# The MLP by half-size products: where raw weights are held, and when the first pair's pieces are formed

## The chip, the core and the metric

The kernel runs on one core of a Trainium2 chip. The core has TensorE (PE), VectorE (DVE), ScalarE (ACT), GpSimd (POOL) and SyncE (SP), each with a queue of its own that is worked off in order, and 16 DMA engines. The metric is the device time of one execution in microseconds. Most executions of a kernel agree within 0.3%.

## The reference, cut to what matters

The program computes two transformer layers with attention and then a block with three mixers. Only its last part is touched by the change: the feed-forward part of the last block, on 512 tokens of width 1024, with an inner width of 4096, all in float32.

```python
h = rmsnorm_2(x, norm_mlp_w[l]) * (1.0 + sc2) + sh2
ff = jnp.square(jax.nn.relu(h @ mlp_w1[l])) @ mlp_w2[l]      # mlp_w1 1024 x 4096, mlp_w2 4096 x 1024
x = x + g2 * ff
return rmsnorm_2(x, final_norm_w)
```

## The kernel before

**Numbers.** Every float32 operand is held as a high part (a copy to fp32r) and a low part (the float32 value minus the high part). A product is three matmuls for each tile: high by high, high by low and low by high. For weights, ACT writes the high part (`wH` for a unit, `pieceH` for a piece) and POOL the low one (`wL`, `pieceL`); DVE writes the low part of some pieces. A low part waits for its high part.

**Units.** A unit is 128 columns of a weight matrix, eight tiles of 128 x 128, loaded as 512 KB. Its raw form lies in one of the two halves of `w32`, by turns, and SP asks for unit u when unit u-2 is split (the semaphore `w_lo` counts split units). Split units lie in 4 slots. ACT and POOL split three units ahead of PE. The matmuls of a unit write a PSUM bank, `G[0]` or `G[1]` by turns.

**The feed-forward part.** It runs in four quarters c = 0 to 3 of 1024 inner columns each. A quarter has eight steps n, one for each unit of the first matrix (units 8c to 8c+7). In a step, PE multiplies unit n. Then ACT takes the relu of the bank, DVE squares it, which gives the bank free (`f_sq`), and forms sums of squares, ACT writes high parts (`hi1`, `sumH`), and POOL and DVE write low parts (`lo1`, `sumL`). PE's unit n+2 needs the bank of unit n.

Then the quarter's product with the second matrix follows by a scheme with seven half-size products for each pair of output columns, where eight would be usual. A pair q (4 a quarter, 15 in all; the last two column blocks are multiplied as ordinary units 32 and 33) is two raw blocks of 512 KB. Seven pieces are formed from them, in the order A11, S1, S2, S4, A12, S3, A22, and held in 10 places by turns. S1, S2 and S4 are formed by DVE in PSUM (`sum_1`, `sum_2`, `sum_4` into banks `O` and `N`), S3 by POOL into `third` (the tile `rms`). ACT writes each piece's high part, POOL the low part of A11, A12, S3 and A22, DVE that of S1, S2 and S4. Raw pairs lie in `wp` (even q) and in `w32` (odd q). In PE's order of a quarter, `first_tiles`, the first three products are `product_1(q)`, `product_5(q)` and `product_1(q + 1)`, then `product_6(q)`. `product_1` takes A11, `product_6` takes S2 and adds into the bank of `product_1`. Before it adds, DVE must have read the bank (`take`, which adds a product to `xT`). At the quarter's end the first half of unit 8 is multiplied between two products of the last pair.

**What sets the order.** The order on each engine is the order of the code in the functions `quarter` and `pieces` of SP, POOL, ACT and DVE; no planner changes it. Before the change, steps 0 to 4 of a quarter end with the split of unit n+3, and steps 5 to 7 end with the pieces of the quarter's first pair. The pieces of pair q+1 begin after step 7. On SP, `quarter` asks for the raw pairs, and for the next quarter's units only when the last pair is split. In quarter 0, DVE has in each step also an `ada_block` (a product with 1024 columns of the modulation matrix, raw in `adaw`, line L1104), and after step 7 the last of these and the sum into `modT`, by which `take` scales.

## Time and profile before

| | us |
|---|---|
| median of 3 runs | 1303.78 (1303.32 to 1304.76) |
| the profiled execution | 1303.05 |
| its span | 1301.3 |
| PE busy | 1237.2 (95%) |
| DVE busy | 813.2 (62%) |
| ACT busy | 718.3 (55%) |
| POOL busy | 448.8 (34%) |
| mean granted clock of TensorE | 0.977 of full speed |

The feed-forward part takes the last third of the span, from about 890 us. Its quarters begin (first matmul of unit 8c) at about 890, 992.4, 1091.5 and 1190.4 us. In a row of a timeline the number in brackets at the end is the time for which the engine stood still before that instruction, and behind the arrow stands what ended it. PE's starts are the better measure of its pace, since matmuls overlap. The times of one execution stand in its rows, so they are compared with its own 1303.05 us.

### The profile page before, as it was taken

What the parts mean: (1) busy time and instruction counts of PE and PEld (TensorE: products, weight loads), DVE (VectorE), ACT (ScalarE), POOL (GpSimd) and SP (SyncE); (2) the same over time, 40 slices, a digit from 0 to 9 for tenths busy, and PEclk for the clock granted to TensorE, in tenths of its full rate; (3) what the DMA queues carried; (4) which work ended last, traced back from release to release, by engine and by line L of the source; (5) the groups of instructions that cost most, each with busy time, mean ns of one, the idle gap of its engine ahead of it and who ended that gap; (6) DMA issues with size and microseconds to landing.
All of it is one profiled execution on the core that took longest, in us unless ns stands there. A gap on an engine that the chain in (4) does not pass through costs nothing.

```text
span 1301.3 us, 20815 instructions
## 1 busy us (share of the span) xinstructions
PE 1237.2 (95%) x7638; PEld 1021.3 (78%) x7638; DVE 813.2 (62%) x1735; ACT 718.3 (55%) x1405; POOL 448.8 (34%) x284
## 2 busy tenths in 40 slices
PE   9999999999999998999999999999878978978977
PEld 8777777778877776896767888889778878878877
DVE  6766667765766666656995466847763453453456
ACT  6666666655456676445678867435422532432432
POOL 0000000005200000434877841233854655655653
PEclk9999999999999999999999999999989989989989
DMA  5312244425232223423220223321512312312311
GB/s 201 115 65 82 81 162 129 129 85 172 86 107 88 82 84 112 139 89 105 73 74 29 71 75 105 130 96 62 199 65 83 113 66 81 113 66 81 113 66 65
DMA packets 38420, 128.21 MB, mean 99 GB/s; under 512 B 4640, under 2 KB 7584, under 8 KB 38320
## 3 DMA queue, kind: packets, MB, share of 16 engines
q1 hardware_dynamic: 35792, 121.91, 28.1%
q10 hardware_dynamic: 2528, 4.98, 1.1%
q8 instruction: 61, 1.00, 0.3%
q14 instruction: 39, 0.32, 0.1%
HBM read 123.43 MB, written 2.13 MB: 96 GB/s over the span
## 4 chain that ended last, share of the span: by engine, by line
PE 71%; issue 8%; DVE 7%; ACT 7%; POOL 5%; DMA 0%; ACTq 0%; DVEq 0%; POOLq 0%
PE G L987 14%; PE G L989 13%; PE G L988 13%; ACT scr L1368 2%; POOL pieceL L634 2%; PE G L2049 2%; PE S L1826 2%; PE G L2050 2%; PE G L2051 2%; PE S L1114 2%; PE O L1175 2%; POOL wL L572 1%; PE T L1154 1%; DVE wL L2761 1%; ACT wH L2198 1%
## 5 line engine op out<-in xcount | busy, mean ns | idle before, releaser
L572 POOL TENSOR_TENSOR wL<-w,wH 128x1024 fp32r<-128x1024 f32 x89 | 216.9, 2442 | 668.0 <-ACT wH L2198 668.0
L987 PE MATMUL G<-hi,wH 128*128 128x512 f32 x968 | 394.8, 408 | 12.0 <-POOL wL L572 11.6
L989 PE MATMUL G<-hi,wL 128*128 128x512 f32 x968 | 380.5, 393 | 0.0
L988 PE MATMUL G<-lo,wH 128*128 128x512 f32 x968 | 380.4, 393 | 0.0
L987 PEld LDWEIGHTS G<-hi,wH 128*128 128x128 f32 x968 | 183.1, 189 | 58.9 <-POOL wL L572 12.7
L989 PEld LDWEIGHTS G<-hi,wL 128*128 128x128 f32 x968 | 183.3, 189 | 40.3
L988 PEld LDWEIGHTS G<-lo,wH 128*128 128x128 f32 x968 | 183.7, 190 | 35.6 <-issue 1.2
L2198 ACT ACTIVATE wH<-w 128x1024 fp32r<-128x1024 f32 x140 | 147.2, 1053 | 101.8 <-DMA w<-weights_dram 72.8
L2761 DVE TENSOR_TENSOR wL<-w,wH 128x1024 fp32r<-128x1024 f32 x51 | 62.3, 1221 | 42.3 <-ACT wH L2198 41.5
L2667 ACT ACTIVATE pieceH<-O 128x512 fp32r<-128x512 f32 x30 | 18.0, 598 | 110.6 <-DVE O L3298 58.7
L3311 DVE SCALAR_TENSOR_TENSOR xT<-G,modT,xT 128x256 f32<-128x256 f32 x60 | 28.9, 482 | 78.6 <-PE G L2051 78.6
L2050 PE MATMUL G<-sumL,pieceH 128*128 128x256 f32 x180 | 52.5, 292 | 0.0
L2051 PE MATMUL G<-sumH,pieceL 128*128 128x256 f32 x180 | 52.4, 291 | 0.0
L2049 PE MATMUL G<-sumH,pieceH 128*128 128x256 f32 x180 | 52.4, 291 | 0.0
L2049 PE MATMUL G<-hi,pieceH 128*128 128x256 f32 x60 | 19.8, 329 | 33.6 <-POOL pieceL L634 32.5
L1142 ACT ACTIVATE scr<-scr,sa 128x256 f32<-128x256 f32 (+2 forms) x64 | 35.2, 557 | 23.7 <-DVE sa L1129 23.7
L1104 DVE CUSTOM_DVE_ANT_0 adaw<-adaw,scr 128x1024 f32<-128x1024 f32 x31 | 45.2, 1457 | 4.3 <-issue 4.0
L1368 ACT ACTIVATE scr<-S,bs,bq 128x128 f32<-128x128 f32 (+1 forms) x64 | 33.6, 534 | 21.7 <-DVE bs L1358 21.7
L634 POOL TENSOR_TENSOR pieceL<-wp,pieceH 128x512 fp32r<-128x512 f32 x24 | 35.3, 1469 | 25.9 <-ACT pieceH L2667 25.9
L646 POOL TENSOR_TENSOR sumL<-sq,sumH 128x256 fp32r<-128x256 f32 (+1 forms) x32 | 33.4, 1046 | 27.5 <-ACT sumH L2706 18.7
L634 POOL TENSOR_TENSOR pieceL<-w,pieceH 128x512 fp32r<-128x512 f32 x21 | 27.5, 1311 | 43.2 <-ACT pieceH L2667 43.2
L2703 ACT ACTIVATE relu<-G 128x512 f32<-128x512 f32 x31 | 18.5, 597 | 40.9 <-PE G L989 37.6
(553 smaller groups left out, 2784.6 us busy)
## 6 DMA issues: line engine op xcount, KB each, us to landing
w<-weights_dram SPq DMA_DIRECT2D x154, 512.0 KB, 3.7
adaw<-ada_dram SPq DMA_DIRECT2D x43, 512.0 KB, 4.1
wp<-weights_dram SPq DMA_DIRECT2D x16, 512.0 KB, 4.6
kd<-c_dram ACTq DMA_DIRECT2D x8, 512.0 KB, 3.7
cbias<-ada_dram SPq DMA_DIRECT2D x5, 512.0 KB, 4.4
xT<-x_dram SPq DMA_DIRECT2D x4, 512.0 KB, 7.8
out_dram<-xT SPq DMA_DIRECT2D x8, 256.0 KB, 2.3
scr<-ca_dram SPq DMA_DIRECT2D x2, 512.0 KB, 5.0
```

What stands on the lines that cost most here:

```text
L572: g.tensor_tensor(wL[:, u.slot], w32[:, u.slot % 2], wH[:, u.slot].bitcast(f32), ALU.subtract).then_inc(w_lo, 1)
L634: g.tensor_tensor(pieceL[:, piece(q, i)], home, pieceH[:, piece(q, i)].bitcast(f32), ALU.subtract).then_inc(piece_lo_g, 1)
L987: mm(home[:, :], whi, H[:, k, :], start=(k == first), stop=False)
L988: mm(home[:, :], whi, L[:, k, :], start=False, stop=False)
L989: last = mm(home[:, :], wlo, H[:, k, :], start=False, stop=(k == final))
L1104: v.tensor_tensor_reduce(out=home, in0=home, in1=copy, scale=1.0, scalar=0.0, op0=ALU.mult, op1=ALU.add, accum_out=modsum[:, b.n:b.n + 1]) ...
L1368: s.activation(pb[:, h * 512 + at:h * 512 + at + w], S[h][:, at:at + w], ACT.Exp, bias=st[:, NEGM, h, q:q + 1], scale=bq[:, n % 2, ROOT, h ...
L2049: mm(home, pieceH[:, at, k, :], high, start=first and k == 0, stop=False, skip_group_check=True)
L2050: mm(home, pieceH[:, at, k, :], low, start=False, stop=False, skip_group_check=True)
L2051: last = mm(home, pieceL[:, at, k, :], high, start=False, stop=(k == 3), skip_group_check=True)
L2198: s.activation(wH[:, u.slot], w32[:, u.slot % 2], ACT.Copy).then_inc(w_hi, 1)
L2761: v.tensor_tensor(wL[:, u.slot], w32[:, u.slot % 2], wH[:, u.slot].bitcast(f32), ALU.subtract).then_inc(w_lo, 1)
```

## The change

Units and pairs share both raw buffers. From quarter 1 on, units 0, 1, 4 and 5 of a quarter lie in `wp`, and units 2, 3, 6 and 7 in `w32`. Where SP waited for the last pair of a quarter to be split and then asked for five units, it now asks for units 8 and 9 when pair q+2 (in `wp`) is split, for 10 and 11 when pair q+3 is split, for 12 and 13 when unit 9 is split and for 14 and 15 when unit 11 is. Pair q of the next quarter follows when its unit 5 is split and pair q+1 when unit 7 is. The semaphores that announce raw data follow the buffer.

(The last hunk is DVE's, at the end of each step.) In a step, the split of unit n+3 stands before the sums' parts: on ACT just behind the relu, on POOL first. The pieces of the first pair are formed in steps 2 to 5, where they were in steps 5 to 7, and A11, S1's and S2's sums of pair q+1 in step 6. At a quarter's end ACT splits units 8, 9 and 10 behind the last piece as before, and in quarter 3 ahead of three squares of the final norm. PE's order is unchanged.

```diff
+        def raw_home(u):
+            c, n = divmod(u.n - UM, 8) if isinstance(u.n, int) else (0, 0)
+            if 0 < c < 4:
+                return (w32 if n // 2 % 2 else wp)[:, n % 2]
+            return w32[:, u.slot % 2]
...
+            def pair_split(q):
+                sp.wait_ge(*mark("piece_sum", 3 * q + 3))
+                sp.wait_ge(*mark("piece_lo_g", 4 * q + 4))
+
             def load_pair(q):
-                if q > 1:
-                    sp.wait_ge(*mark("piece_sum", 3 * (q - 2) + 3))
-                    sp.wait_ge(*mark("piece_lo_g", 4 * (q - 2) + 4))
...
             def quarter(c):
-                for n in range(5, 8):
-                    load_unit(Unit(UM + 8 * c + n))
-                    if c == 0:
-                        load_ada(Block(ADA_M, n - 3))
-                if c == 0:
-                    sp.wait_ge(*mark("lo_mlp", 16))
-                load_pair(4 * c)
+                first = UM + 8 * c
                 if c == 0:
                     for n in range(5, 8):
+                        load_unit(Unit(first + n))
+                        load_ada(Block(ADA_M, n - 3))
+                        if n == 5:
+                            sp.wait_ge(*mark("lo_mlp", 16))
+                            load_pair(0)
+                    for n in range(5, 8):
                         load_ada(Block(ADA_M, n))
-                sp.wait_ge(w_lo, UM + 8 * c + 8)
+                else:
+                    sp.wait_ge(w_lo, first + 6)
+                    load_pair(4 * c)
+                sp.wait_ge(w_lo, first + 8)
                 load_pair(4 * c + 1)
+                pair_split(4 * c)
                 load_pair(4 * c + 2)
-                if c < 3:
-                    load_pair(4 * c + 3)
-                sp.wait_ge(*mark("piece_sum", 3 * (4 * c + 3 - 2 * (c == 3)) + 3))
-                sp.wait_ge(*mark("piece_lo_g", 4 * (4 * c + 3 - 2 * (c == 3)) + 4))
-                for n in range(5 if c < 3 else 2):
-                    load_unit(Unit(UM + 8 * c + 8 + n))
+                pair_split(4 * c + 1)
...
+                load_pair(4 * c + 3)
+                pair_split(4 * c + 2)
+                load_later(first + 8)
+                load_later(first + 9)
+                pair_split(4 * c + 3)
+                load_later(first + 10)
+                load_later(first + 11)
+                sp.wait_ge(w_lo, first + 10)
+                load_later(first + 12)
+                load_later(first + 13)
+                sp.wait_ge(w_lo, first + 12)
+                load_later(first + 14)
+                load_later(first + 15)
...
-                    if n == 5:
+                    if n == 2:
                         sum_1(q)
                         sum_2(q)
-                    if n == 6:
+                    if n == 3:
                         low_of(q, S1)
+                    if n == 4:
                         sum_4(q)
                         low_of(q, S2)
-                    if n == 7:
+                    if n == 5:
                         low_of(q, S4)
+                    if n == 6:
+                        sum_1(q + 1)
+                        sum_2(q + 1)
...
                 take(q, A11)
-                sum_1(q + 1)
                 take(q, S1)
-                sum_2(q + 1)
```

On POOL this is the place from the sums of unit 5 to the second pair, in quarter 1. `sumL` and `lo<-sq` are the low parts of sums for a unit, `pieceL<-wp` those of pair q's A11, A12 and A22, `pieceL<-w` those of pair q+1, and `rms` is S3's sum. Before:

```order
L646 TENSOR_TENSOR sumL<-sq,sumH 128x256
L646 TENSOR_TENSOR sumL<-sq,sumH 128x2x256
L634 TENSOR_TENSOR pieceL<-wp,pieceH 128x512
L640 TENSOR_TENSOR rms<-wp 128x512
L646 TENSOR_TENSOR lo<-sq,hi 128x256
L634 TENSOR_TENSOR pieceL<-wp,pieceH 128x512
L646 TENSOR_TENSOR sumL<-sq,sumH 128x256
L646 TENSOR_TENSOR sumL<-sq,sumH 128x2x256
L634 TENSOR_TENSOR pieceL<-rms,pieceH 128x512
L634 TENSOR_TENSOR pieceL<-wp,pieceH 128x512
L634 TENSOR_TENSOR pieceL<-w,pieceH 128x512
L640 TENSOR_TENSOR rms<-w 128x512
```

And now:

```order
L692 TENSOR_TENSOR sumL<-sq,sumH 128x256
L692 TENSOR_TENSOR sumL<-sq,sumH 128x2x256
L680 TENSOR_TENSOR pieceL<-rms,pieceH 128x512
L680 TENSOR_TENSOR pieceL<-wp,pieceH 128x512
L692 TENSOR_TENSOR lo<-sq,hi 128x256
L680 TENSOR_TENSOR pieceL<-w,pieceH 128x512
L692 TENSOR_TENSOR sumL<-sq,sumH 128x256
L692 TENSOR_TENSOR sumL<-sq,sumH 128x2x256
L686 TENSOR_TENSOR rms<-w 128x512
L680 TENSOR_TENSOR pieceL<-w,pieceH 128x512
```

A11 and the S3 sum of pair q are gone from here to steps 2 and 3, and `pieceL<-w`, A11 of pair q+1, stands ahead of the two `sumL` of unit 7, where it stood as the third instruction behind them.

On ACT this is step 2 and what follows it, in quarter 1, beginning with the relu of unit 2. `wH` is a unit's high part, `hi<-T` and `hi<-sq` are those of the squares and their sums, and `pieceH` those of A11 (from `wp`) and S1 (from bank `O`). Before:

```order
L2703 ACTIVATE relu<-G 128x512
L2714 ACTIVATE hi<-T 128x256
L2715 ACTIVATE hi<-sq 128x256
L2198 ACTIVATE wH<-w 128x1024
L2703 ACTIVATE relu<-G 128x512
L2706 ACTIVATE sumH<-sq 128x256
L2708 ACTIVATE hi<-T 128x512
L2709 ACTIVATE sumH<-sq 128x2x256
L2198 ACTIVATE wH<-w 128x1024
L2703 ACTIVATE relu<-G 128x512
```

And now:

```order
L2752 ACTIVATE relu<-G 128x512
L2248 ACTIVATE wH<-wp 128x1024
L2765 ACTIVATE hi<-T 128x256
L2766 ACTIVATE hi<-sq 128x256
L2717 ACTIVATE pieceH<-wp 128x512
L2717 ACTIVATE pieceH<-O 128x512
L2752 ACTIVATE relu<-G 128x512
L2248 ACTIVATE wH<-w 128x1024
L2757 ACTIVATE sumH<-sq 128x256
L2759 ACTIVATE hi<-T 128x512
L2760 ACTIVATE sumH<-sq 128x2x256
L2717 ACTIVATE pieceH<-N 128x512
```

The unit's high part moved up behind the relu, and the high parts of A11 and S1 of pair q stand between unit 2's sums and the relu of unit 3.

## Rows read from the trace of the kernel before

**Rows 1.** Chain that ended last, of the page, shares of the span by engine.

```profile
PE 71%; issue 8%; DVE 7%; ACT 7%; POOL 5%; DMA 0%; ACTq 0%; DVEq 0%; POOLq 0%
```

**Rows 2.** Waits of PE from 850 us on: waited for, us in total, times, longest us.

```profile
PE G L2049 <- POOL pieceL L634: 32.5, 4, 10.1
PE G L987 <- POOL wL L572: 11.6, 4, 3.5
PE G L2049 <- DVE lo L3343: 1.0, 1, 1.0
PE G L2167 <- POOL wL L572: 1.0, 1, 1.0
```

**Rows 3.** Timeline of PE: start us, us, line, out<-in, idle before and its releaser.

```profile
950.53 0.58 PE L2049 MATMUL G<-hi,pieceH 128*128 128x256 f32 x1 [10.06 <-POOL pieceL L634]
...
992.43 0.50 PE L987 MATMUL G<-hi,wH 128*128 128x512 f32 x1 [3.41 <-POOL wL L572]
...
1091.49 0.50 PE L987 MATMUL G<-hi,wH 128*128 128x512 f32 x1 [3.53 <-POOL wL L572]
```

**Rows 4.** Windows of PE: us, busy, granted clock PEclk, DMA share, GB/s.

```profile
952.00:954.00 2.00, 2.00 (x11) 0.50 0.47 190
```

**Rows 5.** Timeline of PE, single matmuls of the second pair's stage and of quarter 1.

```profile
953.25 0.41 PE L2049 MATMUL G<-sumH,pieceH 128*128 128x256 f32 x1
...
1022.15 0.39 PE L987 MATMUL G<-hi,wH 128*128 128x512 f32 x1
...
1039.16 0.28 PE L2049 MATMUL G<-hi,pieceH 128*128 128x256 f32 x1
...
1040.60 0.28 PE L2049 MATMUL S<-hi,pieceH 128*128 128x256 f32 x1
...
1095.94 0.28 PE L2049 MATMUL G<-sumH,pieceH 128*128 128x256 f32 x1
```

**Rows 6.** Timeline of ACT in quarter 1, units 2, 3, 5, 6 and 7.

```profile
1012.15 0.60 ACT L2703 ACTIVATE relu<-G 128x512 f32<-128x512 f32 x1 [0.89 <-PE G L989]
...
1014.62 1.05 ACT L2198 ACTIVATE wH<-w 128x1024 fp32r<-128x1024 f32 x1
...
1017.59 0.60 ACT L2703 ACTIVATE relu<-G 128x512 f32<-128x512 f32 x1 [1.93 <-PE G L989]
...
1034.76 0.60 ACT L2667 ACTIVATE pieceH<-O 128x512 fp32r<-128x512 f32 x1 [2.17 <-DVE N L3292]
1035.26 0.59 ACT L2703 ACTIVATE relu<-G 128x512 f32<-128x512 f32 x1
...
1040.34 0.59 ACT L2703 ACTIVATE relu<-G 128x512 f32<-128x512 f32 x1
```

**Rows 7.** Timeline of POOL: a unit's low part, and a quarter's last piece.

```profile
1015.74 2.39 POOL L572 TENSOR_TENSOR wL<-w,wH 128x1024 fp32r<-128x1024 f32 x1 [0.20 <-ACT wH L2198]
...
1082.90 1.29 POOL L634 TENSOR_TENSOR pieceL<-w,pieceH 128x512 fp32r<-128x512 f32 x1
```

**Rows 8.** The pair loads' line on SP, time from issue to landing.

```profile
DMA to landing us min/median/max: 3.5/4.5/6.8
```

**Rows 9.** Timeline of DVE: quarter 0's last ada block and modT, then quarter 1.

```profile
944.76 1.70 DVE L1104 CUSTOM_DVE_ANT_0 adaw<-adaw,scr 128x1024 f32<-128x1024 f32 x1
...
946.51 1.10 DVE L3359 TENSOR_TENSOR modT<-modsum,vecT 128x8 f32<-128x8 f32 x1
...
1032.20 1.80 DVE L3288 TENSOR_TENSOR O<-wp 128x512 f32<-128x512 f32 x1
...
1040.97 0.70 DVE L3327 TENSOR_TENSOR T<-relu,G 128x512 f32<-128x512 f32 x1 [1.08 <-ACT relu L2703]
...
1043.44 0.69 DVE L3334 TENSOR_TENSOR lo<-T,hi 128x512 fp32r<-128x512 f32 x1 [0.66 <-ACT hi L2708]
...
1044.65 0.47 DVE L3311 SCALAR_TENSOR_TENSOR xT<-G,modT,xT 128x256 f32<-128x256 f32 x1
1045.04 0.80 DVE L3288 TENSOR_TENSOR O<-w 128x512 f32<-128x512 f32 x1
```

More of the change, by code:

```diff
@@ L348, in pair_home, with pair_raw, raw_here @@
             return w32 if q % 2 else wp
+        def pair_raw(eng, q):
+            for n in range(2):
+                if q % 2:
+                    eng.wait_ge(w_here[n], 16 * (58 + q // 4 * 4 + q % 4 // 2))
+                else:
+                    eng.wait_ge(*mark(f"pair_here{n}", 16 * (1 + q // 4 * 4 + q % 4 // 2)))
+        def raw_home(u):
[3 more added lines that the diff above has]
+            return w32[:, u.slot % 2]
+        def raw_here(u):
+            c, n = divmod(u.n - UM, 8) if isinstance(u.n, int) else (0, 0)
+            if c == 4:
+                return w_here[n], 16 * 71
+            if c > 0 and n // 2 % 2 == 0:
+                return mark(f"pair_here{n % 2}", 16 * (4 * c - 1 + n // 4))
+            if c > 0:
+                return w_here[n % 2], 16 * (56 + 4 * c + n // 4)
+            return w_here[u.slot % 2], u.of_pair * 16 + 16
         def piece(q, i):
@@ L647, in sum_low, with rest @@
                                 ALU.subtract).then_inc(f_sum_lo, 1)
-            def pieces(q):
-                low_of(q, A11, pair_home(q)[:, 0, 0:4])
+            def rest(q):
                 third_sum(q)
@@ L658, in quarter @@
                 for n in range(8):
+                    if n < 5:
+                        split_lo(Unit(UM + 8 * c + 3 + n))
                     if n % 2 == 0:
@@ L2679, in third_high, with rest @@
                 high_of(q, S3, third)
-            def pieces(q):
-                raw_high(q, A11)
+            def rest(q):
                 sum_high(q, S1)
@@ L2715, in quarter @@
                         s.activation(sum_home(c, 1, k), raw_sum[:, 0, :], ACT.Copy).then_inc(sem("f_sum_hi"), 1)
[L2716 to L2718 removed]
+                    if n == 2:
                         raw_high(q, A11)
                         sum_high(q, S1)
[L2721 removed]
+                    if n == 3:
                         sum_high(q, S2)
+                    if n == 4:
                         sum_high(q, S4)
                         raw_high(q, A12)
[L2725 removed]
+                    if n == 5:
                         third_high(q)
                         raw_high(q, A22)
[L2728 removed]
+                    if n == 6:
+                        raw_high(q + 1, A11)
+                rest(q + 1)
                 if c == 3:
                     square_f(0, multiplied(q, A12))
[L2731 removed]
+                raw_high(q + 2, A11)
+                rest(q + 2)
+                if c < 3:
+                    raw_high(q + 3, A11)
+                    rest(q + 3)
+                for n in range(2 if c == 3 else 3):
+                    split_hi(Unit(UM + 8 * c + 8 + n))
                 if c == 3:
@@ L2735, in quarter @@
                     square_f(3, multiplied(q + 1, A22))
-                else:
-                    pieces(q + 3)
-                for n in range(2 if c == 3 else 3):
-                    split_hi(Unit(UM + 8 * c + 8 + n))
             for c in range(4):
```

55 lines of the change are left out of this document (31 added, 24 removed).

## Prediction

> **What bounds the kernel now.** I read the chain of waits first. Matmuls hold 71% of it, and the rest is "issue", ACT, DVE and POOL [rows 1]. TensorE (PE) sets the time, and what can be won are the places where it stands still. The list of PE's waits shows them for the whole feed-forward part [rows 2]: 32.5 us in four waits for POOL's `pieceL`, 11.6 us in four waits for POOL's `wL`, and 1.0 us twice. A reader should see that seven of these ten come at two places that return in each quarter. PE's own timeline gives the places [rows 3]. The wait that ends at 950.53 stands before `product_1(q+1)`, the first product of a quarter's second pair, after two products of the first pair. Those that end at 992.43 and 1091.49 stand before unit 8 of a quarter, which is unit 0 of the next. In all, the waits are 32.5 + 11.6 + 1.0 + 1.0 = 46.1 us.
>
> They cost more than their length. After the wait of 10.06 us the granted clock is 0.50 [rows 4], which is 1.2 GHz of 2.4. At full clock the twelve matmuls of a product take 1.44 us (1039.16 to 1040.60), and after the wait they take 2.72 (950.53 to 953.25) [rows 3, 5], so 1.3 is lost there and about 1.0 in the next product's time, until the clock is back near 955.6. I use 2.3 for each of the four. After the boundary wait, the 12 matmuls from 1091.49 to 1095.94 take 4.45 us [rows 3, 5], where 12 of the 24 in a unit of 5.44 us (the relus of units 2 and 3 lie 1012.15 to 1017.59 [rows 6]) take 2.72: 1.7 lost, three times. Together the stalls cost 46.1 + 4 x 2.3 + 3 x 1.7 = 60.4 us. That is all that the edits can win, since no matmul is removed.
>
> **What the change removes.** The piece wait first. POOL's low part of A11 of pair q+1 now stands in step 6, ahead of unit 7's sums. The sum for S1 and S2 of that pair stands in step 6 on DVE. So `product_1(q+1)` finds its weights. The boundary wait: units 8 and 9 go to the buffer of the pair before last and are asked for when that pair is split, not after the quarter's last piece. Now POOL goes straight from its last piece to `split_lo(8)`. At the second boundary this piece ends at 1084.2 (1082.90 + 1.29) and a split takes 2.4 [rows 7], so 1086.6, and PE is there at 1088.0 (1091.49 - 3.53), 1.4 us later. So all of the 3.4 us goes, at each of the three boundaries. Unit 3's wait in quarter 0 (1.3, the rest of the 11.6) goes because its copies now precede the sums of step 0. The 1.0 at the end of quarter 3 goes for the same reason.
>
> **What it adds in quarters 1 to 3.** Buffer `wp` holds units 4 and 5 of the quarter until unit 5 is split, in step 2. Only then may pair q be asked for, and step 2 ends by waiting for it, on ACT, DVE and POOL alike. These queues are in order: the relu of unit 3 stands behind the pieces on ACT, and the unit 3 square that frees the bank for unit 5 stands behind the sums on DVE. Step by step in quarter 1: relu(2) starts 1012.15; the next ACT start is 0.50 later, the copy takes 1.05 [rows 6]; POOL's subtract takes 2.39 [rows 7], to 1016.2. Loads of pairs landed 4.5 us after their issue at the median [rows 8], so the pair is here at 1020.7. `sum_1` takes 0.80 or, beside a POOL instruction, 1.80 [rows 9]; POOL waits for ACT here, so I take 0.80, to 1021.5. `sum_2` about 0.7, the high part of S1 0.50 to the next start [rows 6], so relu(3) starts at 1022.8 instead of 1017.59. The square starts 0.63 after its relu and takes 0.70 [rows 6, 9], so G[1] is free at 1024.15. Unit 5 started at 1022.15 [rows 5]. The stall is 2.0 us, and with a `sum_1` of 1.80 it is 3.0. The load's own bounds are 3.5 and 6.8 us [rows 8]: 1.0 with the fast sum, 5.3 with the slow one. Does 2.0 lower the clock? In the trace the waits of 1.0 did not and that of 3.41 did, as the 4.45 us for twelve matmuls show [rows 2, 3, 5]. I take 0.5 of the 1.7. Steps 3 to 6 then catch up, since a relu may be some 4 us late before a bank is missed.
>
> The next thing late is `product_6(q)`. It adds into the bank that `take(q, A11)` must have read, and this stands behind unit 7's squares, sums and low part on DVE. A relu that is free starts about 0.9 after its unit's last matmul is out (unit 5 follows at 1022.15, relu(4) is due at 1017.59 + 5.44), so relu(7) stands at 1040.05 for a `product_1(q)` at 1039.16. The low part starts 3.1 later (1040.34 to 1043.44 [rows 6, 9]), the take 0.6 behind it, and it is done 0.47 after that: 1044.2. Three products of 1.44 from 1039.16 end at 1043.5. The stall is 0.9, and I allow 0.7 to 1.3. The longer piece wait had covered it. Per quarter 2.0 + 0.5 + 0.9 = 3.4, three times 10.2.
>
> From there on each piece follows a take that follows a product, as before, at the same distances from PE. There is no PE wait in that phase before [rows 2], so nothing more is paid there.
>
> **What it adds in quarter 0.** Here pair q is loaded early, but every step also has an ada block on DVE (1.70 us for one of them [rows 9]). Pair 1's load stands on SP behind the ada load that waits for block 5. Carrying the durations above through steps 2 to 6 with one such block in each, I put block 5's end at 932.5, pair 1 at 938.2, relu(7) at 938.7, and after two sums of DVE its square at 940.7. So `product_1(q+1)` starts at 940.8, 2.5 us late, and `product_1(q)` was 1.1 late. Unit 7's sums and low part end at 943.2, the ada block at 944.6, `modT` (1.10 [rows 9]) and the take at 946.4. `product_6(q)` starts at 946.5, against 953.25 before [rows 5]: 6.75 us gained of 13.5 (1.3 + 1.0 + 10.06 + 1.1 of low clock). The idle gap of 8 us in two parts will lower the clock again, about 2 us. So 6.75 + 2.0 = 8.75 us stays.
>
> **The sum.** 60.4 - 10.2 - 8.75 = 41.45 us. The profiled execution took 1303.05 us for a span of 1301.3 (1.75 around it), and 1303.05 - 41.45 = 1261.6. The median of the runs, 1303.78, is 0.7 above that execution, so 1262.3, rounded to 1262.
>
> **A rule weighed against the rows.** `sum_1` took 1.80 us at one place, where a POOL subtract ran beside it, and 0.80 at another [rows 9]. The Trainium skill, GPSIMD Engine Reference, section Specifications, says that POOL shares its SBUF interfaces with VectorE and contends with vector instructions that have two SBUF inputs. `sum_1` is such an instruction, and the trace agrees. By that rule alone every moved `sum_1` would cost 1.80, and the time would be 3 us longer, 1265. In the new order POOL's next instruction needs ACT's copy first, so it stands still just then, and the sum above keeps 0.80.
>
> **The rivals.** *A, the raw pair arrives late for step 2.* For it: three engines end step 2 in that wait, one of them with the relu of the next unit behind it. Against it: two banks give slack. With the 6.8 us load and the 1.80 sum the stall is 5.3, and it lowers the clock for 1.7: (5.3 + 1.7 - 2.5) x 3 = 13.5 us more, 1276. *B, nothing new is late.* If ACT and DVE find the pair at once and quarter 0 keeps its order better than I reckon, only the take remains, 3 x 0.9 plus some 3 us in quarter 0: 60.4 - 6 = 54 us gained, 1249. For it: a bank is missed only if its relu is over 4 us late, and the load alone is that long. Against it: the load cannot be asked for before unit 5's split. *C, slower than before: the steps run at ACT's and DVE's pace.* Each hands the other a bank (`first_bank`, `second_bank`), so steps 2 to 6 each may last as their exchange. A step of that kind was long: relu(6) came at 1035.26 [rows 6], where steps of 5.44 from 1017.59 give 1033.9, so it lasted 6.8. At 6.8 five steps cost 6.8 us per quarter, mostly hidden by the slack. It decides against the change when a step passes 8.5 us, since 5 x 3.1 x 4 = 62 us then eat all 60.4; at 9.0 us a step, 72 - 60 = 12 us slower, 1315. Against it: the ada blocks that would make steps so long exist in quarter 0 alone. *D, it doesn't remove the piece wait*, because another input of `product_1(q+1)`, the square of unit 7, comes late too: it ended at 1041.7 (1040.97 + 0.70 [rows 9]), and `product_1(q+1)` is due at 1042.0 (1040.60 + 1.44 [rows 5]). D costs nothing as long as relu(7) is on time, but relu(7) now stands behind pair q+1's load. If that load is 3 us late, each of four quarters gives 3 us back, 1274.
>
> **How the numbers follow.** Forecast 0.52 (1254 to 1269), A 0.20, D 0.10, B 0.13, C 0.05. The range reaches to B's edge and past A: 1249 to 1281. A measurement here tells 0.2% (2.6 us) from no change. All but C lie more than 20 us below, so faster 0.94, same 0.02, slower 0.04.
>
> **What would show it.** Right: no PE wait before `product_1` of pairs 5, 9, 13 nor over 0.5 us at a boundary; a wait of about 2 us before unit 5 of quarters 1 to 3 whose last releaser is DVE's square, with ACT idle before the high part of A11 until the load lands; a wait of about 1 us before `product_6(q)` on DVE's `xT`; some 7 us in quarter 0 around 937 to 947; granted clock 1.00 through nearly all pair stages. Wrong: a wait over 5 us at step 2 or 3 (A), or a `relu` spacing above 8 us in steps 2 to 6 (C), or waits for `wL` at boundaries as before.

## Result and profile after

| | before | after |
|---|---|---|
| median, us | 1304.27 (1303.32 to 1305.66, 4 runs) | 1262.6 (1261.96 to 1264.08, 4 runs) |
| the profiled execution | 1303.05 | 1261.96 |
| its span | 1301.3 | 1260.2 |
| PE busy | 1237.2 | 1226.8 |
| mean granted clock | 0.977 | 0.996 |

The ratio is 0.9681, with a 95% interval of [0.9665, 0.9698]: 41.7 us faster. PE executes the same 7638 matmuls in both; it is busy 10.4 us less because it runs at full clock for longer.

The chain that ended last in the changed kernel, against [rows 1]:

```profile
PE 75%; ACT 7%; DVE 7%; issue 6%; DMA 2%; POOL 1%; SPq 0%; ACTq 0%; DVEq 0%; POOLq 0%
```

The matmuls' share rose from 71% to 75% and POOL's fell from 5% to 1%. DMA is new with 2%, the raw pair for which step 2 now waits. The waits of PE from 850 us on, against [rows 2] (waited for, us in total, times, longest us):

```profile
PE G L1037 <- DVE T L3381: 6.5, 5, 1.7
PE G L2099 <- issue: 4.3, 3, 3.5
PE G L2099 <- POOL pieceL L680: 2.5, 1, 2.5
PE G L2099 <- DVE lo L3397: 1.6, 1, 1.6
```

46.1 us of waits became 14.9. L1037 was L987, and L2099 was L2049. No wait for `wL` is left, and one for `pieceL`, in quarter 0. PE's timeline says where these 14.9 us lie, against [rows 3] (in brackets the wait, and what ended it):

```profile
939.25 0.36 PE L2099 MATMUL G<-hi,pieceH 128*128 128x256 f32 x1 [1.62 <-DVE lo L3397]
...
945.12 0.52 PE L2099 MATMUL G<-hi,pieceH 128*128 128x256 f32 x1 [2.45 <-POOL pieceL L680]
...
951.49 0.36 PE L2099 MATMUL G<-sumH,pieceH 128*128 128x256 f32 x1 [3.49 <-issue]
...
1018.00 0.47 PE L1037 MATMUL G<-hi,wH 128*128 128x512 f32 x1 [1.52 <-DVE T L3381]
...
1104.09 0.47 PE L1037 MATMUL G<-hi,wH 128*128 128x512 f32 x1 [1.71 <-DVE T L3381]
```

The first three are quarter 0: before `product_1(q)`, `product_1(q+1)` and `product_6(q)`. The last two are unit 5 of quarters 1 and 2 (quarter 3 has one of 1.56). `product_6(q)` waits 0.47 in quarter 2 and 0.38 in quarter 3. Quarter 0 has two more for a bank, 0.33 before unit 3 (908.49) and 1.34 before unit 5 (920.96). Where the profile names "issue" for `product_6`, DVE's rows below show what it waited for.

The clock, in windows of PE (us, busy, granted clock, DMA share, GB/s), against [rows 4]:

```profile
946.00:948.00 2.00, 1.99 (x10) 0.50 0.00 0
...
952.00:954.00 2.00, 2.00 (x11) 0.50 0.00 0
...
1016.00:1018.00 2.00, 0.48 (x4) 1.00 0.00 0
1018.00:1020.00 2.00, 2.00 (x9) 1.00 0.00 0
```

In quarter 0 the clock falls to 0.50 (1.2 GHz) twice. Around the wait of 1.52 in quarter 1 it stays at 1.00 (2.4 GHz), and so it does at every wait of quarters 1 to 3.

By the spacing of the relus of units 8c (ACT's timeline; the last stage ends with the span), in us:

| stage | before | after | gained | forecast |
|---|---|---|---|---|
| quarter 0 and its boundary | 99.60 | 92.14 | 7.46 | 11.05 |
| quarter 1 | 99.06 | 85.91 | 13.15 | 11.4 |
| quarter 2 | 98.90 | 86.57 | 12.33 | 11.4 |
| quarter 3 to the end | 102.07 | 92.97 | 9.1 | 7.6 |

The forecast column divides the prediction's own terms: waits and clock of a stage, less 3.4 a quarter or 8.75 in quarter 0. The relu of unit 0 stands 0.94 us later than before (902.61 against 901.67), in code that the change does not touch. It lay between 900.8 and 904.8 in the profiled executions of this study, so a difference of up to 4 us between single spans need not be the effect of an edit. From that relu on, two profiled executions of the changed kernel lasted 357.6 and 358.5 us, 0.9 apart. The experiments below are compared by medians, by PE's waits, and where it matters by the span from that relu on.

### The profile page after: what moved, and what is told of

It reads as the page before. It is cut to its first block, busy times and chain, and to the rows that moved or that the text cites. A ratio compares the mean times of both kernels' runs of the same rounds, so it can differ in the third digit from the quotient of the medians.

```text
span 1260.2 us, 20816 instructions
## 1 busy us (share of the span) xinstructions
PE 1226.8 (97%) x7638; PEld 1010.3 (80%) x7638; DVE 816.9 (65%) x1735; ACT 716.3 (57%) x1405; POOL 447.7 (36%) x284
## 4 chain that ended last, share of the span: by engine, by line
PE 75%; ACT 7%; DVE 7%; issue 6%; DMA 2%; POOL 1%; SPq 0%; ACTq 0%; DVEq 0%; POOLq 0%
PE G L1037 14%; PE G L1039 13%; PE G L1038 13%; PE G L2099 2%; PE G L2100 2%; PE G L2101 2%; ACT scr L1418 2%; PE S L1164 2%; PE O L1225 2%; PE S L1876 1%; PE T L1204 1%; ACT wH L2248 1%; DVE wL L2815 1%; PE S L2100 1%; PE S L2101 1%
## 5 line engine op out<-in xcount | busy, mean ns | idle before, releaser
L618 POOL TENSOR_TENSOR wL<-w,wH 128x1024 fp32r<-128x1024 f32 x77 | 189.7, 2468 | 678.0 <-ACT wH L2248 677.9
L1037 PE MATMUL G<-hi,wH 128*128 128x512 f32 x968 | 393.0, 406 | 6.9 <-DVE T L3381 6.5
L1037 PEld LDWEIGHTS G<-hi,wH 128*128 128x128 f32 x968 | 182.1, 188 | 54.5 <-issue 18.6
L2248 ACT ACTIVATE wH<-w 128x1024 fp32r<-128x1024 f32 x128 | 134.7, 1054 | 80.5 <-DMA w<-weights_dram 48.9
L2099 PE MATMUL G<-sumH,pieceH 128*128 128x256 f32 x180 | 51.5, 286 | 4.4 <-issue 4.3
L1154 DVE CUSTOM_DVE_ANT_0 adaw<-adaw,scr 128x1024 f32<-128x1024 f32 x31 | 48.2, 1555 | 1.9 <-issue 1.8
L2099 PEld LDWEIGHTS G<-sumH,pieceH 128*128 128x128 f32 x180 | 34.7, 193 | 5.3 <-issue 5.2
```

Of the source, the lines that this page charges most:

```text
L618: g.tensor_tensor(wL[:, u.slot], raw_home(u), wH[:, u.slot].bitcast(f32), ALU.subtract).then_inc(w_lo, 1)
L1037: mm(home[:, :], whi, H[:, k, :], start=(k == first), stop=False)
L1154: v.tensor_tensor_reduce(out=home, in0=home, in1=copy, scale=1.0, scalar=0.0, op0=ALU.mult, op1=ALU.add, accum_out=modsum[:, b.n:b.n + 1]) ...
L2099: mm(home, pieceH[:, at, k, :], high, start=first and k == 0, stop=False, skip_group_check=True)
L2248: s.activation(wH[:, u.slot], raw_home(u), ACT.Copy).then_inc(w_hi, 1)
```

## The experiments

The theory is the prediction's: the gain is the sum of three separate waits, each with a loss of clock behind it, and what remains is one wait per quarter for the raw pair, with quarter 0 on DVE's pace. The rival is that the waits overlap, or that one of the edits does nothing. "After" means the changed kernel, 1262.6 us. Each ratio is to the kernel before, with its 95% interval.

**The second pair's pieces back behind step 7.**

```diff
-                    if n == 6:
-                        low_of(q + 1, A11, pair_home(q + 1)[:, 0, 0:4])
+                low_of(q + 1, A11, pair_home(q + 1)[:, 0, 0:4])
                 rest(q + 1)
...
-                    if n == 6:
-                        raw_high(q + 1, A11)
+                raw_high(q + 1, A11)
                 rest(q + 1)
...
-                    if n == 6:
-                        sum_1(q + 1)
-                        sum_2(q + 1)
...
                 take(q, A11)
+                sum_1(q + 1)
                 take(q, S1)
+                sum_2(q + 1)
```

> The changed kernel, but A11 and the sums for S1 and S2 of pair q+1 are formed after step 7 again. Theory 1 (the step-6 pieces remove the piece wait): in quarters 1 to 3 POOL's low part of A11 ends some 4.2 us after product_1(q+1) is due, and this covers the wait of about 0.45 us before product_6; with about 2.3 us of low clock that makes 3 x 6 = 18 us, and quarter 0 about 0, since relu(7) is then free of pair 1's load: 1281 us. Rival (the gain came from the shared raw buffers and the earlier unit copies): under 2 us more, 1264 us at most.

Measured: 1276.91 us (1276.15 to 1277.45), ratio [0.9782, 0.9814]. PE's waits and its clock at the one in quarter 1:

```profile
PE G L2098 <- POOL pieceL L680: 15.6, 4, 4.1
```

```profile
1038.00:1040.00 2.00, 1.35 (x6) 0.50 0.00 0
```

The wait is back in all four quarters, 3.8 to 4.1 us each, and the clock falls at each of them. It takes 14.3 us from the gain: 13.1 us more of waits for pieces, 4.3 less before `product_6` (the longer wait covers it), and the rest is clock. The wait is not 8.1 us as before, since the first pair's pieces now stand in steps 2 to 5 and POOL, ACT and DVE come to the second pair sooner.

The expectation was 1281, and the 4 us between lie in quarter 0. By the spacing of the relus, quarters 1 to 3 took 6.2, 5.5 and 5.8 us longer than in the changed kernel, 17.5 in all where 18 were expected; quarter 0 took 89.42 us where the changed kernel took 92.14, 2.7 less. So the second pair's pieces in step 6 are worth 17.5 us in quarters 1 to 3 and cost 2.7 in quarter 0, where the relu of unit 7 stands behind the pair's late load. No run kept them in step 6 for quarters 1 to 3 alone.

**The next quarter's units asked for only behind the last piece.**

```diff
                 pair_split(4 * c + 2)
-                load_later(first + 8)
-                load_later(first + 9)
                 pair_split(4 * c + 3)
+                load_later(first + 8)
+                load_later(first + 9)
```

> The changed kernel, but units 8 and 9 are asked for only when the quarter's last pair is split. Theory 1 (the earlier request removes the wait at the boundary): POOL's last piece ends 3.0 us before PE needs unit 8, landing 3.7, copy 1.06, low part 2.4 make a wait of 4.2 us, and 1.7 us of low clock, three times: 1280 us. Rival (PE is held at the boundary by something else, or the slack of 1.4 us that was forecast was not real): under 5 us more in all.

Measured: 1280.87 us (1279.75 to 1281.27), ratio [0.9809, 0.9842]. The waits:

```profile
PE G L1037 <- POOL wL L618: 10.4, 3, 3.6
```

The boundary waits are back as they were, and the clock falls at each, 18.3 us in all. So the earlier request is worth about 6 us a boundary, where the prediction had 3.4 + 1.7 = 5.1. The waits before unit 5 and in quarter 0 are 0.7 us longer here too, and the last of the three falls of the clock lasted longer than the other two.

**A step's copies for unit n+3 back at its end.**

```diff
                 for n in range(8):
-                    if n < 5:
-                        split_lo(Unit(UM + 8 * c + 3 + n))
                     if n % 2 == 0:
                         sum_low(c, n // 2, 1)
...
                         sum_low(c, n // 2, 2)
                         sum_low(c, n // 2, 3, 2)
+                    if n < 5:
+                        split_lo(Unit(UM + 8 * c + 3 + n))
```

That is POOL's part; on ACT `split_hi` moves in the same way behind the step's high parts.

> The changed kernel, but unit n+3 is split behind the sums of its step again. Theory 1 (in steps 2 of quarters 1 to 3 PE waits for the chain unit 5's split, pair load, sums, relu of unit 3): the split ends 1.75 us later, so the wait before unit 5 grows from 1.5 to 3.3 us, and a clock drop of 1.7 may follow: 5 to 10 us more and 1 us in quarter 0, 1269 to 1274 us. Rival (moved copies only matter for unit 3 of quarter 0): 1263.6 us.

Measured: 1276.88 us (1275.78 to 1279.59), ratio [0.9789, 0.9821], 3 us above the expected range. PE's waits, then the one of quarter 1 and the clock around it:

```profile
PE G L1037 <- DVE T L3381: 12.3, 4, 3.9
...
PE G L1037 <- POOL wL L618: 2.5, 2, 1.3
```

```profile
1022.39 0.76 PE L1037 MATMUL G<-hi,wH 128*128 128x512 f32 x1 [3.44 <-DVE T L3381]
```

```profile
1022.00:1024.00 2.00, 1.61 (x4) 0.50 0.00 0
```

The waits grew as expected: raw unit 5 is split later, the pair is asked for later, and unit 5's product waits 3.4 to 3.9 us where it waited 1.5 to 1.7. The clock, which the expectation had as a possibility, falls at each of the three; after 1.5 to 1.7 us it stays at 1.00. The upper end of the expectation already holds these falls at 1.7 us each. What lies above it is spread: the three waits grew by 6.2 us and not by 5.4, the second of the falls lasted longer than the other two, and quarter 0 took 2.1 us more by its relus and not 1, with waits of 1.30 and 1.19 for `wL`. So this edit, which looks like a detail, is worth 14 us, mostly because it keeps the new wait short and the clock up.

**The first pair's pieces one step later in quarters 1 to 3** (steps 3 to 6 in place of 2 to 5), on POOL, ACT and DVE:

```diff
+LATER = 1
...
-                    if n == 2:
+                    m = n - LATER if c else n
+                    if m == 2:
                         low_of(q, A11, pair_home(q)[:, 0, 0:4])
-                    if n == 3:
+                    if m == 3:
...
```

> The changed kernel, but in quarters 1 to 3 the first pair's pieces are formed in steps 3 to 6, not 2 to 5. Theory 1 (ACT and DVE hold unit 3's relu and square while they wait for the pair's load): the pair lands about 0.4 us before relu(3)'s step ends, so the three waits of 1.5 to 1.7 us before unit 5 go, 4.8 us in all, and POOL has 4.6 us of work in step 6, less than a step of 5.44: 1258 us. Rival (POOL or ACT has no room in step 6, so the wait moves to product_1(q+1)): 1262 to 1266 us.

Measured: 1256.39 us (1255.08 to 1260.07), ratio [0.9622, 0.9675], 6.2 us less than after. Its waits of PE:

```profile
PE G L2101 <- issue: 4.6, 1, 4.6
PE G L2101 <- POOL pieceL L681: 2.4, 1, 2.4
```

These two, 1.6 before `product_1(q)` and 1.6 in quarter 0's first steps are all that is left of the waits of the feed-forward part, and they lie in quarter 0. In quarters 1 to 3 no wait of PE is listed, neither before unit 5 nor before `product_6`, and no new one came. ACT and DVE have the same work in these quarters as before the edit. So the wait before unit 5 was the raw pair's landing inside step 2 and not their pace (rival C): the relus of units 2 and 3 of quarter 1, which lay 10.9 us apart, now lie 5.44 apart. By the relus, quarters 1 to 3 are 1.8, 2.45 and 2.1 us shorter than in the changed kernel, 6.3 in all, which is what its waits there cost.

**The last ada block and `modT` in step 6 of quarter 0, ahead of the second pair's sums.**

```diff
+                    if c == 0 and n == 6:
+                        ada_block(dve, Block(ADA_M, 7))
+                        dve.wait_ge(sem("ada_summed"), 48)
+                        link(v.tensor_tensor(modT[:, 40:48], modsum[:, 40:48], vecT[:, 40:48], ALU.add))
...
-                if c == 0:
-                    ada_block(dve, Block(ADA_M, 7))
-                    dve.wait_ge(sem("ada_summed"), 48)
-                    link(v.tensor_tensor(modT[:, 40:48], modsum[:, 40:48], vecT[:, 40:48], ALU.add))
```

> The changed kernel, but in quarter 0 DVE does the last ada block and modT in step 6, ahead of the sums of pair 1, where it stands still for 2.7 us waiting for that pair. Theory 1 (product_6 of pair 0 waits for the take, which stands behind the ada block and modT): the take comes 3.5 us sooner, while the sums of pair 1 come up to 0.5 us later: 3 us less, 1259.6 us. Rival (product_6 waits for the low sums of POOL): no change, 1262.6 us.

Measured: 1258.89 us (1257.07 to 1262.48), ratio [0.9641, 0.9682]. The wait before `product_6` in quarter 0 fell from 3.49 to 0.90:

```profile
948.45 0.55 PE L2099 MATMUL G<-sumH,pieceH 128*128 128x256 f32 x1 [0.90 <-issue]
```

The work fits into time in which DVE stood still: the changed kernel's DVE was idle for 2.74 us before `sum_1` of pair 1. Where it stood, the block and `modT` took 2.30 and 1.10 us, and here 1.59 and 0.17, and `sum_1` still waits 1.04 us for the pair. The last section has what made them slow.

**The take of A11 ahead of unit 7's low part, in quarters 1 to 3.**

```diff
+TAKE_C = 1
...
+                        if n == 7 and TAKE_C <= c:
+                            take(q, A11)
                         dve.wait_ge(sem("f_hi"), 8 * c + n + 1)
...
-                take(q, A11)
+                if c < TAKE_C:
+                    take(q, A11)
```

> The changed kernel, but in quarters 1 to 3 DVE takes A11's product between unit 7's sums and its low part, where DVE stands still 0.67 us for ACT. Theory 1 (product_6 waits for that take): the waits of 0.4 to 0.5 us before product_6 go, 1 us or a little more in all: 1261.5 us. Rival (it waits for the unit's low part or for POOL): 1262.6 us or more. The difference is near what 3 rounds can tell, so the wait in the trace decides.

Measured: 1261.21 us (1260.24 to 1263.04), ratio [0.9655, 0.9701]. The waits before `product_6` in quarters 2 and 3 are gone from PE's timeline. By the median it is 1.4 us less; the intervals of the two ratios overlap, so the time alone does not show it.

**Pair 1 asked for ahead of ada block 7's load in quarter 0.**

```diff
-                    for n in range(5, 8):
+                    for n in range(5, 7):
                         load_ada(Block(ADA_M, n))
...
                 load_pair(4 * c + 1)
+                if c == 0:
+                    load_ada(Block(ADA_M, 7))
```

> The changed kernel, but in quarter 0 SP asks for pair 1 ahead of the last ada load. Theory 1 (relu(7) of quarter 0 stands behind the high part of A11 of pair 1, whose load stands behind an ada load that waits for block 5): pair 1 is here some 6 us sooner, relu(7) comes at about 939.5 and not 943.5, the wait of 2.5 us before product_1(1) goes, and the one before product_6(0) stays near 3 us, as the take moves with relu(7): 3 to 4 us less, 1259 us. Rival (DVE's own work in step 6 sets relu(7)'s square): under 1 us.

Measured: 1260.71 us (1259.74 to 1261.95), ratio [0.9654, 0.9697]. The relu of unit 7 came earlier, and the time before `product_6` was longer:

```profile
940.31 0.59 ACT L2754 ACTIVATE relu<-G 128x512 f32<-128x512 f32 x1
```

```profile
950.13 0.55 PE L2101 MATMUL G<-sumH,pieceH 128*128 128x256 f32 x1 [4.68 <-issue]
```

After, this relu stood at 943.53. Counted from each execution's relu of unit 0 (903.55 here, 902.61 after), it comes 4.2 us earlier, as expected. But the median fell by 1.9 us only, under the 3 to 4 expected: PE did not wait before `product_1(q+1)`, but 1.2 us longer before `product_6`, because DVE still has the ada block and `modT` in front of the take.

**Three of these together** (one step later, the take, pair 1's load):

> The changed kernel with three edits together: pieces one step later in quarters 1 to 3, the take ahead of unit 7's low part there, and pair 1's load ahead of the last ada load. If theory 1 holds they add up: 4.8 + 1.2 + 3.5 = 9.5 us less, 1253 us. If the waits hide one another, less than the largest alone gives and a new wait shows in the trace.

Measured: 1254.6 us (1252.1 to 1256.8), ratio [0.9598, 0.9651]. From the relu of unit 0 on the span is 9.7 us shorter than after, and alone the three edits gave 5.6 (one step later), 3.2 (pair 1's load) and 0.9 (the take) by the same measure: they add up.

**Work in the place of a wait.** The next two ask about the clock alone. The kernel before, with extra matmuls whose results are not used:

```diff
+            def filler(q, count, bank):
+                for n in range(count):
+                    mm(bank[:, HALF[0]], pieceH[:, piece(q, A11), n % 4, :], hi1[:, n % 4, HALF[0]], start=True, stop=True)
...
                 product_5(q)
+                filler(q, 76 if c == 0 else 56, S[1])
                 product_1(q + 1)
```

> The kernel before, with extra matmuls of 256 columns (into a bank of PSUM that is free there; their results are not used, the output stays as it was) between product 5 of a pair and product 1 of the next: 76 in quarter 0 (about 9.1 us of TensorE at full clock) and 56 in each of quarters 1 to 3 (about 6.7 us), so that TensorE computes while the next pair's pieces are late. The four waits for POOL's pieces (8.1 us each before) shrink to what the extra matmuls leave, the pieces come as late as before. Theory 1 (a wait of this length costs its length and then some 2.3 us more, through a granted clock of .50 when TensorE starts again): the clock stays at 1.00 at the four places and the run takes 4 x 2.2 = 9 us less than the kernel before, about 1294.5 us, though TensorE has more to do. Rival (the clock falls there for another cause, or the slow stretch costs nothing because something else is late): no gain, 1303 us or more.

Measured: 1294.72 us (1293.77 to 1296.12) against 1303.82 for the kernel before, measured beside it, ratio [0.9922, 0.9954]. The waits, the second pair's first matmul in quarter 0, and the clock there, where the kernel before has 0.50 [rows 4]:

```profile
PE G L987 <- POOL wL L572: 10.7, 4, 3.2
PE G L2049 <- POOL pieceL L634: 3.6, 4, 1.3
```

```profile
949.72 0.39 PE L2049 MATMUL G<-hi,pieceH 128*128 128x256 f32 x1 [1.04 <-POOL pieceL L634]
```

```profile
952.00:954.00 2.00, 2.00 (x20) 1.00 0.04 12
```

244 more matmuls, 9.1 us faster. The waits for pieces fell by 28.9 us and the extra work is about 29.3 us (0.12 each), so nothing was gained there. The clock stayed at 1.00 at all four places, and the 9.1 us are what four falls of the clock cost: 2.3 us each, or 1.5 to 2.5 by the ends of the ratio's interval. That is the prediction's term, and here it is taken by itself, but for the boundaries: their waits were 0.9 us less in all, and the clock was low for longer behind one of them. The Trainium skill, TensorE: Matmul & The Clock Gate, section Part 1: The HAM clock gate, puts the penalty of the ramp from the low to the full clock under 1% of a typical kernel's span. For the four falls taken away here this run agrees (0.6%, by its interval 0.5 to 0.8%). With the three at the boundaries, 14.3 us by the prediction's terms, it is an estimated 1.1% of this kernel, the size of a real edit.

The three edits together, with 34 such matmuls before `product_6` in quarter 0:

> The three edits of x9 together, and before product 6 of pair 0 in quarter 0, where x9 still waits 4.7 us and then runs at a clock of .50, 34 extra matmuls of 256 columns (4.1 us at full clock, results not used, output unchanged). Theory 1 (the wait lowers the clock): the wait becomes work, the clock stays at 1.00 and 1.5 to 2 us are saved: 1253 us against x9's 1254.6. Rival (the clock falls anyway): no difference from x9, 1254.6 us. If the extra matmuls end after the piece arrives: up to 0.5 us slower than theory 1 says.

Measured: 1251.9 us (1250.99 to 1254.73), ratio [0.9595, 0.9626]. In the trace the wait is 0.66 in place of 4.69:

```profile
949.20 0.36 PE L2104 MATMUL G<-sumH,pieceH 128*128 128x256 f32 x1 [0.66 <-issue]
```

The clock behind the place of the wait, here and then without the extra matmuls, where the wait ended at 951.36:

```profile
950.00:952.00 2.00, 2.00 (x19) 1.00 0.00 0
```

```profile
952.00:954.00 2.00, 2.00 (x11) 0.50 0.00 0
```

The medians differ by 2.7 us, but they were not measured side by side, and their ratios' intervals overlap. From the first of PE's waits in quarter 0, the same instruction in both (it ended at 910.66 and 908.42), to the end the spans are 342.0 and 340.8, 1.3 us less, somewhat under the 1.5 to 2 expected. The direction agrees with the theory; the time does not prove it, the clock's rows do.

**The changed kernel once more,** as the measure for the two with extra matmuls:

> The changed kernel once more, as it is, on the same chip as the two with extra matmuls, so that they are compared in one call: 1262.6 us as before, within 1.5 us.

Measured: 1263.61 us (1262.63 to 1265.05), ratio [0.968, 0.9712]. That is 1.0 us above its first median.

**One step later, the take, and the last ada block in step 6:**

> Three edits together that were run singly: the pieces of the first pair one step later in quarters 1 to 3 (alone 1256.4 us, 6.2 less than the change), the product's take ahead of unit 7's low part (alone 1261.2, 1.4 less), and in quarter 0 the last ada block with modT in step 6 (alone 1258.9, 3.7 less). Theory 1 (the four waits of quarter 0 and the ones of quarters 1 to 3 are separate, so the gains add): 1262.6 - 6.2 - 1.4 - 3.7 = 1251.3 us, and where single runs' errors of about 1 us each overstate them, up to 1253; no wait of PE of 2 us or more but the one before product 1 of pair 1 (2.6). Rival (the gains overlap, or ada block 7 in step 6 delays unit 7 so that its loss shows once the rest is gone): 1254.5 us or more, with a wait over 3 us before product 1 or product 6 in quarter 0.

Measured: 1252.77 us (1250.35 to 1254.22), ratio [0.9593, 0.962]. The waits of PE that are left, 6.8 us, all in quarter 0:

```profile
PE G L2102 <- POOL pieceL L682: 2.8, 1, 2.8
...
PE G L2102 <- issue: 0.8, 1, 0.8
```

The gains add up again within their errors: 9.8 us by the medians, where the single medians sum to 11.3, and 9.6 from the relu of unit 0 on, where they sum to 8.7 (5.6, 0.9 and 2.2). This version has no extra matmuls, and is 50.7 us faster than the kernel before (1303.51, measured beside it).

The three edits of the change do not add up in this way. Taken back singly they cost 14.3, 18.3 and 14.3 us, 46.9 in all, more than the 41.7 that they brought together. The first two remove waits of the kernel before. The third mostly keeps a wait short that the first two brought with them.

## Why the prediction was right, and where its sizes were off

The forecast was 1262.0 and the runs gave 1262.6. The mechanism held in quarters 1 to 3 and in the main in quarter 0, but two terms were off in opposite directions and made up for each other; that the sum came so close is luck.

*What bounds the kernel.* Right. The time lies in PE's waits and the clock behind them. The clock's share, 2.3 us for each wait for a piece, was worked out from two rows; the extra matmuls measured it as 9.1 us for four (6.0 to 10.2).

*What the change removes.* Right but for quarter 0's first steps. No wait before `product_1(q+1)` in quarters 1 to 3, none at a boundary. The wait for `wL` before unit 3 of quarter 0, 1.29 before, is gone as forecast, but 0.33 for a bank is left there, and 1.34 before unit 5 is new. POOL goes from the last piece to the split of unit 8 without a gap (start us, us, then [rows 7]'s columns):

```profile
982.67 1.30 POOL L680 TENSOR_TENSOR pieceL<-w,pieceH 128x512 fp32r<-128x512 f32 x1
983.93 4.78 POOL L618 TENSOR_TENSOR wL<-wp,wH 128x1024 fp32r<-128x1024 f32 x2
```

*The wait for the raw pair in step 2.* Right in its chain, a little large in its size. The same rows of quarter 1 as the prediction built them from [rows 6 to 9], now with the pair's request on SP:

```profile
1005.63 0.60 ACT L2752 ACTIVATE relu<-G 128x512 f32<-128x512 f32 x1 [1.83 <-PE G L1039]
...
1014.56 0.63 ACT L2717 ACTIVATE pieceH<-wp 128x512 fp32r<-128x512 f32 x1 [6.37 <-issue]
...
1016.53 0.59 ACT L2752 ACTIVATE relu<-G 128x512 f32<-128x512 f32 x1
```

```profile
1007.25 2.41 POOL L618 TENSOR_TENSOR wL<-wp,wH 128x1024 fp32r<-128x1024 f32 x1 [1.08 <-ACT wH L2248]
```

```profile
1009.69 0.80 SPq L555 DMA_DIRECT2D wp<-weights_dram  x2
```

```profile
1014.57 0.70 DVE L3342 TENSOR_TENSOR O<-wp 128x512 f32<-128x512 f32 x1 [6.22 <-DMA wp<-weights_dram]
1015.30 0.70 DVE L3346 TENSOR_TENSOR N<-O,wp 128x512 f32<-128x512 f32 x1
...
1017.15 0.70 DVE L3381 TENSOR_TENSOR T<-relu,G 128x512 f32<-128x512 f32 x1 [1.15 <-ACT relu L2752]
```

ACT and DVE both stand still until the pair has landed, 4.9 us after its request, and the relu of unit 3, PE's bank, follows behind them: PE starts unit 5 at 1018.00, when DVE's square is out. ACT's row says "issue", and only DVE's names the DMA: the releaser of a wait is to be read on the engine that shows it. From relu(2) to `sum_1` it took 8.94 us where the prediction had 8.55, and `sum_1` took 0.70 in step 2 of all three quarters, about the 0.80 that the prediction chose, and not the 1.80 of the rule that it weighed, since POOL had nothing to do there. In step 6 POOL was at work, and there `sum_1` took 1.09, 3.07 and 0.91. The stall is 1.5 to 1.7 and not 2.0. It does not touch the clock, where the prediction took 0.5. And `product_6` waits 0, 0.47 and 0.38 and not 0.9 (the prediction's own 1044.2 less 1043.5 is 0.7): in quarter 1 relu(7) started 0.2 us after `product_1(q)`, at 1034.63, where the prediction had 0.9; in quarter 2 the `sum_1` of 3.07 stood before unit 7's square. So the term of 10.2 us measured 5.6 by the waits (1.52 + 1.71 + 1.56 + 0.47 + 0.38), and 6.3 by the relus against the run without them.

*Quarter 0.* Right in three of its places, without the first two, and too small in its size: 8.75 us were to stay. Measured: 9.2 us of waits (0.33 + 1.34 + 1.62 + 2.45 + 3.49), and the clock at half from 945.2 to 948.6 and from 952.0 to 955.4, which is about 3.1 us of matmul time, 12.3 us together. The first two waits, 1.67 us, stood in the prediction at nothing; the one before unit 5 is step 2 again, with `sum_1` behind an ada block of 2.67 us in place of a load. The clock cost 1.1 us more than forecast. What made `product_6(q)` late is in DVE's rows:

```profile
934.17 2.33 DVE L1154 CUSTOM_DVE_ANT_0 adaw<-adaw,scr 128x1024 f32<-128x1024 f32 x1
...
942.99 0.70 DVE L3342 TENSOR_TENSOR O<-w 128x512 f32<-128x512 f32 x1 [2.74 <-issue]
...
947.42 2.30 DVE L1154 CUSTOM_DVE_ANT_0 adaw<-adaw,scr 128x1024 f32<-128x1024 f32 x1
...
949.76 1.10 DVE L3417 TENSOR_TENSOR modT<-modsum,vecT 128x8 f32<-128x8 f32 x1
950.90 0.48 DVE L3365 SCALAR_TENSOR_TENSOR xT<-G,modT,xT 128x256 f32<-128x256 f32 x1
```

The prediction carried 1.70 us for each ada block. Those of steps 2 to 5 took 2.67, 1.38, 1.66 and 2.33, 1.2 us more in all, and block 7 took 2.30. Block 5, whose end lets SP go on, ended at 936.5 and not at 932.5. Pair 1 was asked for at 936.9, landed 6.1 us later, at 943.0 and not at 938.2, and the take began at 950.9 and not at 945.9. Of each of these differences 0.94 us is the later relu of unit 0. The ada blocks explain 1.2 of the remaining 3.1 us at block 5; for the rest the prediction gives its steps only as a whole, so which of them was too short stays open. That chain, from block 5 by pair 1's load to the take, is the term that was sized too small. Its two halves were then taken away singly, by the earlier request for pair 1 and by the earlier ada block.

*The sum.* 60.4 - 5.6 - 12.3 = 42.5 us against the 41.45 forecast, and 41.1 by the spans, with 0.94 of it lost ahead of the changed part. The error of one term, +3.6, and of the other, -4.6, nearly cancel. That the time came out within 1 us is therefore luck; by itself the working was good to some 4 us.

*The rivals.* A (a wait over 5 us at step 2) did not occur. C, the steps at ACT's and DVE's pace throughout, did not occur either, though the sign that the prediction named for it did: the relus of units 2 and 3 lay 8.98, 10.90, 11.08 and 10.93 us apart in the four quarters. The prediction's own working has 10.65 there (1012.15 to 1022.8), so a single step over 8 us could not tell C from the forecast. The five steps from relu(2) to relu(7) tell them apart: 29.0 to 29.2 us in quarters 1 to 3 after, 28.2 to 28.9 before, where C needs over 42. D's condition, relu(7) held by pair q+1's load, did occur in quarter 0 alone. It is part of the 12.3 us, and with the pieces back behind step 7 quarter 0 was 2.7 us shorter. B, nothing new late, is not what this kernel does, but it is what the last version comes near: 1252.8 us.

## What to carry to other kernels

Count an idle gap of the bounding engine at its length and then ask whether it is long enough to lower the clock: here gaps of 1.8 us and less did not, and those of 3.0 us and more did, for some 2 us more each. When a wait can't be removed, work moved into it can be worth more than its own length. And where a load's buffer comes free late, put the work that needs the data one step later, when nothing on the chain needs it at once: that was worth 6 us here and cost nothing.

## What was not expected of the hardware

**VectorE and GpSimd take turns.** DVE instructions that read two SBUF operands took different times: the ada block (128x1024) from 1.22 to 2.67 us, `sum_1` (128x512) from 0.70 to 3.07. In the feed-forward part of the changed kernel 18 of these two kinds started while a POOL instruction ran. All but one ended 0.56 us (`sum_1`) or 1.09 us (ada block) after that POOL instruction, and POOL's next one took 0.45 or 1.0 us longer than usual. For the ada block of step 5, 934.17 + 2.33 = 936.50, and POOL's first row ends at 934.12 + 1.30 = 935.42; its second takes 1.29 elsewhere:

```profile
934.12 1.30 POOL L692 TENSOR_TENSOR sumL<-sq,sumH 128x512 fp32r<-128x512 f32 x1 [0.41 <-ACT sumH L2760]
935.38 2.28 POOL L680 TENSOR_TENSOR pieceL<-rms,pieceH 128x512 fp32r<-128x512 f32 x1
```

So what such an instruction loses depends on how much of POOL's running one is left. The one exception is the longest, in quarter 2, DVE and then POOL:

```profile
1118.12 3.07 DVE L3342 TENSOR_TENSOR O<-w 128x512 f32<-128x512 f32 x1
1121.23 0.70 DVE L3346 TENSOR_TENSOR N<-O,w 128x512 f32<-128x512 f32 x1
```

```profile
1117.35 1.32 POOL L680 TENSOR_TENSOR pieceL<-wp,pieceH 128x512 fp32r<-128x512 f32 x1
1118.60 0.78 POOL L692 TENSOR_TENSOR lo<-sq,hi 128x256 fp32r<-128x256 f32 x1
1119.30 1.33 POOL L680 TENSOR_TENSOR pieceL<-w,pieceH 128x512 fp32r<-128x512 f32 x1
```

This sum was issued while the first POOL instruction ran, and ended 0.6 us after the third: 1119.30 + 1.33 = 1120.63, and 1118.12 + 3.07 = 1121.19. Why it was passed over twice is not shown. `sum_2`, with an operand in PSUM, took its usual 0.70. It goes the other way too: POOL's `lo<-sq`, 0.73 alone, took 1.82 where it started together with an ada block, which then took its 1.22. So the two don't slow each other by a factor; in these rows one waits until the other's instruction is done. The Trainium skill, GPSIMD Engine Reference, section Specifications, has the contention, and the rows agree and show its form. No experiment took it apart.

**Short waits leave the clock alone.** Behind the waits of 1.0 to 1.8 us the granted clock stayed at 1.00 in every profile here. At every one of 3.0 us and more (2.99 the shortest) it was at 0.50: it fell while PE waited or within 1.5 us after, and in two places it was low already. Those of 2.4 to 2.8 lie between: it fell at or after 2.45 (the changed kernel), 2.38, 2.42, 2.64 twice, 2.75 and 2.78, and not after 2.47 (with the copies late). All of these stand before `product_1(q+1)` in quarter 0, after another wait of 1.5 to 1.6 us and 3.4 us of work, so the length of the one wait need not be all that counts. Nor does it always fall at once: the windows of the last version around its wait of 2.78, which ended at 945.93 (us, busy, granted clock, DMA share, GB/s):

```profile
944.00:946.00 2.00, 0.07 (x1) 1.00 0.60 238
946.00:948.00 2.00, 2.00 (x12) 0.73 0.01 2
948.00:950.00 2.00, 1.23 (x6) 0.50 0.00 0
```

PE started at full clock and lost it about a microsecond later: a mean of 0.73 over two microseconds is full clock for 0.9 and half for 1.1. Behind the wait of 3.49 in the changed kernel it was half a microsecond. The same kernel differs here from one execution to the next: in a second profile of the changed kernel the clock fell 1.4 us after a wait of 2.42 and stayed low through the next wait, to 5 us behind it. So one row at the end of a wait doesn't tell its cost; the windows behind it do.
